# Odd attention: four weight groups in every second step in place of two in each

## The chip, the cores and the metric

The kernel runs on one NeuronCore of one Trainium2 chip. The metric is device time in microseconds (us) of one execution, the median over several runs of the same program. Everything is fp32 outside; inside, the big products are made from pairs of fp32r operands (a head and a tail), three matmuls each.

The engines are named as the profile names them: PE is TensorE's matmul, PEld its weight load, DVE is VectorE, ACT ScalarE, POOL GpSimd, SP the queue that loads the weights from memory.

## The reference, cut to what matters

A two-layer trunk on one sequence of 512 tokens, 1024 features. Layer 0 ("even") mixes with gated DeltaNet and differential attention, layer 1 ("odd") with 16-head attention, and each has a gated MLP behind it. The change touches the odd layer's attention only:

```
h = rmsnorm(x, odd_norm_mix)
cq, ck, cv = split_cols(h @ odd_w_qkv, (1024, 1024, 1024))      # 16 heads of 64
# chunks of 64 tokens; each attends to its own chunk and the 8 before it: here all that came earlier
s = einsum("bqhd,bkhd->bhqk", q_c, k_b) * 64**-0.5 + bias
p = softmax(where(valid, s, -inf))
o = einsum("bhqk,bkhd->bqhd", p, v_b)
x = x + o_c @ odd_w_out
```

With 512 tokens the band of nine chunks reaches everything before, so the mask is block-causal. In blocks of 128 queries, block b (0 to 3) has (b + 1) * 128 keys.

## The kernel before

**Pairs and steps.** The 16 heads go as eight pairs (pair 0 to pair 7). `attention("odd", i, ...)` on each engine handles one pair: eight score tiles, item t = (head m = t % 2, query block b = t // 2), and four blocks of the product with the values. PE runs twelve steps, t = 0 to 11:

- t < 8: the scores s_t, two matmuls (L846, L847) with 128, 256, 384 or 512 columns, into bank R0 for even t and R1 for odd t. DVE reads them, adds the bias and takes the maximum (L1655); ACT takes the exponential (L1183); DVE multiplies by the reciprocal sum, which gives the tile `pn` (L1684, L1689).
- t = 1: `vt`, four transposes of the value tile `vf` (L853) into bank R2. ACT copies them to `av` (L1187).
- t >= 2: `t{z}` with z = t - 2, that is z // 2 + 1 transposes of `pn` (L863), into bank R2 as well. ACT copies each to `pT` (in the trace `pT` or `qr`, L1195). Bank R2 has one user at a time: the transposes of z wait for ACT's copy of z - 1.
- even t >= 4: the values' product of block (t - 4) // 2 (L874) into bank R3.

In the text below tr_z stands for the transposes of item z.

**The fill.** While a pair's attention runs, PE also computes the next pair's projection q, k, v, as 24 *groups* of three matmuls with 512 columns (L619, L620, L621), one group for each of the eight slices of the 1024 inputs and each of three output tiles. They come from a generator, `features`; `run(fill, n)` takes the next n groups. Before the change each step t < 8 runs two groups and each step from 8 on one; what is left runs behind step 11. For pair 7 the fill is the output projection's first 21 groups (`out_terms`, tiles oh, ol). Inside a step the order is: scores, vt, fill, transposes, values' product. Each engine executes its own queue strictly in the order of the program, with semaphores between the engines.

**What the start of a pair waits for.** At steps 8 and 9 and behind step 9, ACT and DVE empty the next pair's projection: DVE writes `aq`, `ak`; ACT splits the next weights (`wh`, L373), DVE their tails (`wl`, L377); ACT writes `qs` and `kh` (L1087 to L1089), DVE `qs`'s tails, one for each head of the pair (L1384, x2, semaphore `q_tail`), POOL `kl` (L549, `k_tail`); and then DVE writes `vf` (L1413, semaphore `acc_free1`). The scores s_0 and s_1, which belong to different heads, each wait for their own head's tails, and vt waits for `vf`. Behind `vf` DVE writes the previous pair's `ol` and a weight tail, and only then reads s_0.

Of the kernel before, what the change touches and what calls it, by code (L numbers as in the profile page):

```python
# [157 lines left out]
def build(nc, T, out):  # L158

    ctx = ExitStack()  # L160
    with ctx:
# [5 lines left out]
        def sem(name):  # L167
            if name not in sems:
                sems[name] = ctx.enter_context(nc.semaphore(name))
            return sems[name]  # L170
# [170 lines left out]
        def read(eng, phase, job, i):  # L341

            b, n = BANK.use(phase, job, i)
            eng.wait_ge(sem(f"R{b}_read"), n + 1)
# [262 lines left out]
        def _(pe):  # L607
            def job(phase, name, i, first=True):
                b, n = BANK.use(phase, name, i)
                if not (isinstance(n, int) and n == 0):  # L610
                    pe.wait_ge(sem(f"R{b}_read"), n)
                return R[b]

            def done(ins, phase, name, i):
                b, _ = BANK.use(phase, name, i)
                ins.then_inc(sem(f"R{b}_full"), 1)
# [33 lines left out]
            def run(gen, n=1000):  # L650
                for _ in range(n):
                    if next(gen, 0) == 0:
                        return

            def token_sums(r, c0, squares):

                for b in range(NB):
                    last = nc.tensor.matmul(r[:, c0 + b:c0 + b + 1], squares[:, b * P:(b + 1) * P], ones[:, 0:1],  # L658
                                            start=True, stop=True)
                return last  # L660
# [161 lines left out]
            def rope_products(i):  # L822
                for n, nm_ in enumerate(("rot_q", "rot_k")):
                    pe.wait_ge(sem("acc_free0"), 2 * i + (2 * UNIT["diff"] + n + 3))
                    r = job("diff", nm_, i)
                    done(nc.tensor.matmul(r[:, :], cblk(C_PERM), qr[n][:, :], start=True, stop=True),
                         "diff", nm_, i)

            def attention(ph, i, fill, more=True):

                diff = ph == "diff"
                items = [(m, b) for b in range(NB) for m in (0, 1)]
                o = None
                per = 4 if diff else 8
                for t in range(8 + 4):
                    if t < 8:
                        m, b = items[t]
                        r = job(ph, f"s{t}", i)
                        if b == 0:
                            n = i if diff else i + NH  # L840
                            if m == 0:
                                pe.wait_ge(sem("kl_zero"), 2 if diff else 4)
                            for name in ("q_tail", "k_copy", "k_tail"):
                                pe.wait_ge(sem(name), 2 * n + (m + 1))
                        w = slice(0, (b + 1) * P)
                        nc.tensor.matmul(r[:, w], qs[m][:, b * P:(b + 1) * P], kh[m][:, w], start=True, stop=False)  # L846
                        done(nc.tensor.matmul(r[:, w], qs[m][:, b * P:(b + 1) * P], kl[m][:, w], start=False,  # L847
                                              stop=True), ph, f"s{t}", i)
                    if t == 1:
                        pe.wait_ge(sem("acc_free1"), 2 * i + (2 * UNIT[ph] + 2))  # L850
                        r = job(ph, "vt", i)
                        for b in range(NB):
                            last = nc.tensor.transpose(r[:, b * P:(b + 1) * P], vf[:, b * P:(b + 1) * P], ident)  # L853
                        done(last, ph, "vt", i)
                    run(fill, 2 if t < 8 else 1)

                    z = (t - 3) // 2 if diff and (t - 3) % 2 == 0 else t - 2 if not diff else -1
                    if 0 <= z < per:
                        b = z if diff else items[z][1]
                        pe.wait_ge(sem("pn_" + ph), per * i + z + 1)  # L860
                        r = job(ph, f"t{z}", i)
                        for k in range(b + 1):
                            last = nc.tensor.transpose(r[:, k * P:(k + 1) * P], pn[z % 2][:, k * P:(k + 1) * P], ident)  # L863
                        done(last, ph, f"t{z}", i)

                    b = (t - 4) // 2 if t % 2 == 0 else -1
                    if 0 <= b < NB:
                        if o is None:
                            o = job(ph, "pv", i)
                        read(pe, ph, f"t{b if diff else 2 * b + 1}", i)  # L870
                        for k in range(b + 1):
                            for m in (0,) if diff else (0, 1):
                                rows_ = slice(0, P) if diff else half[m]
                                last = nc.tensor.matmul(o[rows_, b * P:(b + 1) * P], av[:, k, rows_],  # L874
                                                        pT[2 * m + b % 2][:, k * P:(k + 1) * P],
                                                        start=(k == 0), stop=(k == b))
                        if b == NB - 1:
                            done(last, ph, "pv", i)
                        else:
                            last.then_inc(sem("pv_" + ph), 1)  # L880
                    if t == 9 and diff and more:
                        rope_products(i)
                run(fill)
                if diff:
                    pe.wait_ge(sem("sqo_diff"), i + 1)
                    r = job(ph, "oc", i)
                    done(token_sums(r, 0, osd), ph, "oc", i)
                    pe.wait_ge(sem("do_diff"), i + 1)
                    r = job(ph, "ro", i)
                    done(nc.tensor.matmul(r[:, :], ones, osd[:, :], start=True, stop=True), ph, "ro", i)  # L890
# [71 lines left out]
            with pe.Fori(0, NH - 1) as i:  # L962
                attention("diff", i, attn_units(i + (UNIT["diff"] + 1)))

            def heads_wait(k):
                pe.wait_ge(sem("oc_tail" if k < NH else "o_tail"), k % NH + 1)

            attention("diff", NH - 1, out_terms(UNIT["out0"], (0, 1, 2, 4, 5, 6, 3), KD - 1, heads_wait), more=False)
            out_rest(UNIT["out0"], KD - 1, heads_wait)
            mlp_layer(0, 1)  # L970
# [6 lines left out]
            with pe.Fori(0, NPAIR - 1) as i:  # L977
                attention("odd", i, attn_units(i + (UNIT["odd"] + 1)))
# [857 lines left out]
```

## Time and profile before

| | us |
|---|---|
| median of 3 runs | 1458.46 (1452.70 to 1458.87) |
| the profiled execution, whole | 1460.56 |
| its span | 1458.9 |
| PE busy | 1391.2 (95%) |
| DVE busy | 843.6 (58%) |
| ACT busy | 619.7 (42%) |
| POOL busy | 181.2 (12%) |
| mean granted clock of PE | 0.964 |

The span is what the profiler saw between the first and the last instruction; the whole execution's time is 1.7 us longer. Odd attention, steps 0 to 11 of eight pairs, takes from 834 us to some 1038 us of the span, 25.6 us a pair. In the timeline an instruction's row gives its start, its duration, engine, line, operation, tiles and shapes; where its engine stood idle before it, the idle time and who ended it follow in brackets. Matmuls overlap in the pipe, so the distance between two starts is what one costs, not its duration.

### The profile page before, as it was taken

What the parts mean: (1) busy time and instruction counts of PE and PEld (TensorE: products, weight loads), DVE (VectorE), ACT (ScalarE), POOL (GpSimd) and SP (SyncE); (2) the same over time, 40 slices, a digit from 0 to 9 for tenths busy, and PEclk for the clock granted to TensorE, in tenths of its full rate; (3) what the DMA queues carried; (4) which work ended last, traced back from release to release, by engine and by line L of the source; (5) the groups of instructions that cost most, each with busy time, mean ns of one, the idle gap of its engine ahead of it and who ended that gap; (6) DMA issues with size and microseconds to landing.
All of it is one profiled execution on the core that took longest, in us unless ns stands there. A gap on an engine that the chain in (4) does not pass through costs nothing.

```text
span 1458.9 us, 19831 instructions
## 1 busy us (share of the span) xinstructions
PE 1391.2 (95%) x6775; PEld 1138.7 (78%) x6775; DVE 843.6 (58%) x1235; ACT 619.7 (42%) x865; POOL 181.2 (12%) x177
## 2 busy tenths in 40 slices
PE   5979999899989999999999999999999999999996
PEld 4769878677767888888888777777778888888874
DVE  5666675566655666435555556667556664355542
ACT  4333232355543444223334566666444442233342
POOL 1031033011222100000001312122220000000011
PEclk9979979899989999999999999999999999999998
DMA  6421011012323642333313422324223323334132
GB/s 190 147 58 30 20 39 30 15 44 58 115 58 102 171 131 73 107 108 92 110 54 90 129 71 82 89 70 112 76 58 98 103 72 107 109 87 114 55 90 58
DMA packets 218642, 124.80 MB, mean 86 GB/s; under 512 B 6048, under 2 KB 215435, under 8 KB 218341
## 3 DMA queue, kind: packets, MB, share of 16 engines
q1 hardware_dynamic: 213744, 112.54, 27.4%
q0 software_dynamic: 3664, 11.58, 2.8%
q8 instruction: 29, 0.48, 0.1%
q10 hardware_dynamic: 1188, 0.08, 0.1%
q14 instruction: 17, 0.13, 0.0%
HBM read 119.94 MB, written 9.48 MB: 89 GB/s over the span
## 4 chain that ended last, share of the span: by engine, by line
PE 86%; DVE 5%; ACT 5%; issue 3%; DMA 1%; POOL 0%; ACTq 0%; DVEq 0%; SPq 0%; POOLq 0%
PE acc L619 24%; PE acc L620 23%; PE acc L621 23%; PE R L720 4%; ACT wh L373 2%; PE R L874 2%; PE R L863 1%; PE R L846 1%; PE R L658 1%; PE R L847 1%; PE R L740 1%; DVE wl L377 1%; DVE cta L1362 1%; PE R L718 1%; DMA xin<-in_x 1%
## 5 line engine op out<-in xcount | busy, mean ns | idle before, releaser
L619 PE MATMUL acc<-mh,wh 128*128 128x512 f32 x1120 | 456.4, 408 | 9.5 <-DVE ml L1315 5.4
L621 PE MATMUL acc<-mh,wl 128*128 128x512 f32 x1120 | 442.0, 395 | 0.0
L620 PE MATMUL acc<-ml,wh 128*128 128x512 f32 x1120 | 441.4, 394 | 0.0
L377 DVE TENSOR_TENSOR wl<-raw,wh 128x2048 fp32r<-128x2048 f32 x116 | 251.8, 2171 | 135.8 <-ACT wh L373 135.7
L373 ACT ACTIVATE wh<-raw 128x2048 fp32r<-128x2048 f32 x116 | 210.1, 1811 | 145.7 <-PE acc L621 144.3
L619 PEld LDWEIGHTS acc<-mh,wh 128*128 128x128 f32 x1120 | 213.9, 191 | 56.0 <-issue 9.2
L621 PEld LDWEIGHTS acc<-mh,wl 128*128 128x128 f32 x1120 | 213.1, 190 | 46.2
L620 PEld LDWEIGHTS acc<-ml,wh 128*128 128x128 f32 x1120 | 214.0, 191 | 41.5 <-issue 2.6
L494 POOL TENSOR_TENSOR ssum<-ssum,sq 128x512 f32<-128x512 f32 x32 | 52.0, 1624 | 716.8 <-ACT sq L1007 716.1
L619 PE MATMUL acc<-ah,wh 128*128 128x512 f32 x352 | 137.7, 391 | 0.4 <-DVE wl L377 0.3
L621 PE MATMUL acc<-ah,wl 128*128 128x512 f32 x352 | 137.0, 389 | 0.0
L620 PE MATMUL acc<-al,wh 128*128 128x512 f32 x352 | 137.0, 389 | 0.0
L1757 DVE SCALAR_TENSOR_TENSOR cta<-cb,pv,cta 128x512 f32<-128x512 f32 x88 | 66.2, 752 | 74.1 <-ACT cta L1254 67.7
L1183 ACT ACTIVATE pr<-ns,nm 128x128 f32<-128x128 f32 (+3 forms) x96 | 53.9, 561 | 76.3 <-DVE nm L1655 53.3
L1254 ACT ACTIVATE cta<-cb,pv 128x512 f32<-128x512 f32 x44 | 35.9, 817 | 103.8 <-DVE cb L1750 103.6
L619 PEld LDWEIGHTS acc<-ah,wh 128*128 128x128 f32 x352 | 66.0, 188 | 16.5 <-issue 2.3
L621 PEld LDWEIGHTS acc<-ah,wl 128*128 128x128 f32 x352 | 66.1, 188 | 14.0
L620 PEld LDWEIGHTS acc<-al,wh 128*128 128x128 f32 x352 | 66.1, 188 | 13.2
L1777 DVE TENSOR_TENSOR x<-x,acc 128x512 f32 (+1 forms) x32 | 22.0, 688 | 72.6 <-PE acc L621 72.3
L1260 ACT ACTIVATE ah<-pd 128x512 f32 x44 | 27.8, 632 | 69.6 <-DVE pd L1766 69.6
L1655 DVE CUSTOM_DVE_ANT_0 ns<-R,gb 128x128 f32<-128x128 f32 (+3 forms) x64 | 30.7, 489 | 44.6 <-PE R L847 44.6
L619 PE MATMUL acc<-oh,wh 128*128 128x512 f32 x128 | 53.3, 416 | 3.0 <-DVE ol L1719 3.0
(285 smaller groups left out, 1780.5 us busy)
## 6 DMA issues: line engine op xcount, KB each, us to landing
raw<-in_ffn_w_in SPq DMA_DIRECT2D x88, 512.0 KB, 5.0
raw<-in_even_w_in SPq DMA_DIRECT2D x24, 512.0 KB, 5.2
raw<-in_ffn_w_out SPq DMA_DIRECT2D x32, 384.0 KB, 4.1
raw<-in_ffn_w_out SPq DMA_DIRECT2D x32, 320.0 KB, 3.6
raw<-in_odd_w_qkv SPq DMA_DIRECT2D x16, 512.0 KB, 4.5
rel_bias_extended<-rel_bias_rows POOLq DMA_DIRECT2D x16, 320.0 KB, 4.0
raw<-in_even_w_out SPq DMA_DIRECT2D x8, 512.0 KB, 4.6
raw<-in_odd_w_qkv SPq DMA_DIRECT2D x16, 256.0 KB, 3.1
```

The costliest lines, as they stand in the source:

```text
L373: nc.scalar.activation(wh[s][:, 0:n], raw[s][:, 0:n], ACT.Copy).then_inc(sem(f"w_head{s}"), 1)
L377: nc.vector.tensor_tensor(wl[s][:, 0:n], raw[s][:, 0:n], wh[s][:, 0:n].bitcast(F32), ALU.subtract).then_inc(sem(f"w_tail{s}"), 1)
L494: pool.tensor_tensor(ssum[:, :], ssum[:, :], sq[s][:, :], ALU.add).then_inc(sem("ssum"), 1)
L619: nc.tensor.matmul(o, ah_, bh_, start=first, stop=False)
L620: nc.tensor.matmul(o, ah_, bl_, start=False, stop=False)
L621: return nc.tensor.matmul(o, al_, bh_, start=False, stop=last)
L720: last = nc.tensor.matmul(r[:, t], lhs, triu if b is triu else b[:, t], start=True, stop=True)
L874: last = nc.tensor.matmul(o[rows_, b * P:(b + 1) * P], av[:, k, rows_], pT[2 * m + b % 2][:, k * P:(k + 1) * P], start=(k == 0), stop=(k = ...
L1183: A(pr[t % 2][:, 0:w], ns[t % 2][:, 0:w], ACT.Exp, bias=nm[:, t:t + 1], scale=-1.0, accum_out=rs[:, t:t + 1]).then_inc(sem("exp_" + ph), 1)
L1254: A(cta[s][:, :], cb[s][:, ALPHA - 2:ALPHA - 2 + S], ACT.Identity, bias=pv[:, bass.ds(j + (PV_CB + JF * layer), 1)], scale=pv[:, bass.ds(j ...
L1655: free(V.tensor_tensor_reduce(out=ns[t % 2][:, 0:w], in0=r[:, 0:w], in1=bias, scale=-1.0, scalar=3e38, op0=ALU.add, op1=ALU.min, accum_out ...
L1757: V.scalar_tensor_tensor(out=cta[s][:, :], in0=cb[s][:, o:o + S], scalar=pv[:, bass.ds(j + (w0 + JF * tap), 1)], in1=cta[s][:, :], op0=ALU ...
```

## The change

The number of groups that a step takes from the fill. Before: two in each of the steps 0 to 7, one from step 8 on. After: for differential attention (`diff`) the same; for odd attention none in steps 0, 2, 4, 6, four in steps 1, 3, 5, 7, and one from step 8 on. The sum over the first eight steps stays 16.

```
-                    run(fill, 2 if t < 8 else 1)
+                    run(fill, 2 if diff and t < 8 else 1 if t >= 8 else 4 * (t % 2))
```

Only PE's queue changes; those of DVE, ACT, POOL and SP are the same. The start of a pair on PE, before (here pair 7, whose fill reads oh and ol; the other pairs read the same with mh and ml), from s_0's second matmul to s_2's first, with the semaphores that each waits for:

```order
L847 MATMUL R<-kl,qs 128x128
L619 MATMUL acc<-oh,wh 128x512 [waits R3_read,acc_free0,w_tail0]
...
L621 MATMUL acc<-oh,wl 128x512
L846 MATMUL R<-kh,qs 128x128 [waits k_copy,k_tail,q_tail,R1_read]
L847 MATMUL R<-kl,qs 128x128
L853 MATMUL R<-cst,vf 128x128 [waits R2_read,acc_free1]
L853 MATMUL R<-cst,vf 128x128 x3
L619 MATMUL acc<-oh,wh 128x512 [waits R3_read]
...
L846 MATMUL R<-kh,qs 128x256 [waits R0_read]
```

and after:

```order
L847 MATMUL R<-kl,qs 128x128
L846 MATMUL R<-kh,qs 128x128 [waits k_copy,k_tail,q_tail,R1_read]
L847 MATMUL R<-kl,qs 128x128
L853 MATMUL R<-cst,vf 128x128 [waits R2_read,acc_free1]
L853 MATMUL R<-cst,vf 128x128 x3
L619 MATMUL acc<-oh,wh 128x512 [waits R3_read,acc_free0,w_tail0]
...
L846 MATMUL R<-kh,qs 128x256 [waits R0_read]
L847 MATMUL R<-kl,qs 128x256
L863 MATMUL R<-cst,pn 128x128 [waits R2_read,pn_odd]
```

The two groups between s_0 and s_1 have moved behind vt, and the two between s_2 and tr_0 behind s_3. The second place is steps 3 and 4 on PE, from tr_1 to s_5, before:

```order
L863 MATMUL R<-cst,pn 128x128 [waits R2_read,pn_odd]
L846 MATMUL R<-kh,qs 128x384 [waits R0_read]
L847 MATMUL R<-kl,qs 128x384
L619 MATMUL acc<-oh,wh 128x512
...
L621 MATMUL acc<-oh,wl 128x512
L863 MATMUL R<-cst,pn 128x128 [waits R2_read,pn_odd]
L863 MATMUL R<-cst,pn 128x128
L874 MATMUL R<-pT,av 64x128 [waits R2_read,R3_read]
L874 MATMUL R<-qr,av 64x128
L846 MATMUL R<-kh,qs 128x384 [waits R1_read]
```

and after:

```order
L863 MATMUL R<-cst,pn 128x128 [waits R2_read,pn_odd]
L846 MATMUL R<-kh,qs 128x384 [waits R0_read]
L847 MATMUL R<-kl,qs 128x384
L863 MATMUL R<-cst,pn 128x128 [waits R2_read,pn_odd]
L863 MATMUL R<-cst,pn 128x128
L874 MATMUL R<-pT,av 64x128 [waits R2_read,R3_read]
L874 MATMUL R<-qr,av 64x128
L846 MATMUL R<-kh,qs 128x384 [waits R1_read]
L847 MATMUL R<-kl,qs 128x384
L619 MATMUL acc<-oh,wh 128x512
```

Between tr_1 and tr_2, which use bank R2 one after the other, two groups stood before; now only s_4 does. Steps 5 and 6 (tr_3, s_6, tr_4) moved in the same way.

## Rows read from the trace of the kernel before

**Rows 1.** One pair by window: length, busy time of each engine, granted clock, DMA
```profile
860.40:886.00 25.60, 25.44 (x154) 20.14 (x153) 16.87 (x41) 17.07 (x35) 5.57 (x7) 1.00 0.29 81
```

**Rows 2.** PE's waits in the odd stage: total us, times, longest
```profile
PE R L874 <- ACT qr L1195: 1.1, 7, 0.2
PE R L846 <- DVE nm L1655: 0.7, 1, 0.7
```

**Rows 3.** Timeline of PE, pair 1: start, us, engine, line, operation
```profile
860.47 0.22 PE L846 MATMUL R<-kh,qs 128*128 128x128 f32 x1
...
860.64 0.44 PE L619 MATMUL acc<-mh,wh 128*128 128x512 f32 x1
...
862.26 0.62 PE L853 MATMUL R<-cst,vf 128*128 128x128 f32 x4
...
867.42 0.27 PE L863 MATMUL R<-cst,pn 128*128 128x128 f32 x1
...
867.88 0.39 PE L619 MATMUL acc<-mh,wh 128*128 128x512 f32 x1
...
870.40 0.39 PE L619 MATMUL acc<-mh,wh 128*128 128x512 f32 x1
...
871.78 0.38 PE L863 MATMUL R<-cst,pn 128*128 128x128 f32 x2
...
872.47 0.39 PE L619 MATMUL acc<-mh,wh 128*128 128x512 f32 x1
```

**Rows 4.** Timeline of DVE, start of pair 1
```profile
857.73 3.36 DVE L1384 TENSOR_TENSOR qs<-aq,qs 64x512 fp32r<-64x512 f32 x2
861.13 0.69 DVE L1413 TENSOR_TENSOR vf<-acc,rstd 128x512 f32<-128x512 f32 x1
```

**Rows 5.** Timeline of ACT, pair 1
```profile
864.58 0.58 ACT L1187 ACTIVATE av<-R 128x512 f32<-128x512 f32 x1
...
867.72 0.28 ACT L1195 ACTIVATE qr<-R 128x128 f32<-128x128 f32 x1 [0.24 <-PE R L863]
...
872.20 0.39 ACT L1195 ACTIVATE qr<-R 128x256 f32<-128x256 f32 x1
...
879.08 1.91 ACT L373 ACTIVATE wh<-raw 128x2048 fp32r<-128x2048 f32 x1
880.88 0.59 ACT L1195 ACTIVATE qr<-R 128x512 f32<-128x512 f32 x1
```

**Rows 6.** Timeline of PE's weight loads: s_0 of pair 0, last values' product of pair 1
```profile
834.08 0.19 PEld L846 LDWEIGHTS R<-kh,qs 128*128 128x128 f32 x1 [1.08 <-DVE qs L1384]
...
881.52 0.13 PEld L874 LDWEIGHTS R<-pT,av 128*64 128x64 f32 x1 [0.59 <-ACT qr L1195]
```

**Rows 7.** Timeline of PE, start of pair 0
```profile
834.08 0.33 PE L846 MATMUL R<-kh,qs 128*128 128x128 f32 x1 [0.65 <-DVE qs L1384]
...
834.36 0.44 PE L619 MATMUL acc<-mh,wh 128*128 128x512 f32 x1
...
835.80 0.31 PE L846 MATMUL R<-kh,qs 128*128 128x128 f32 x1
...
836.58 0.66 PE L853 MATMUL R<-cst,vf 128*128 128x128 f32 x4 [0.36 <-DVE vf L1413]
```

**Rows 8.** Timeline of DVE, start of pair 0
```profile
835.76 0.69 DVE L1413 TENSOR_TENSOR vf<-acc,rstd 128x512 f32<-128x512 f32 x1
```

**Rows 9.** Timeline of ACT and of PE, step 2 of pair 7
```profile
1019.36 0.58 ACT L1187 ACTIVATE av<-R 128x512 f32<-128x512 f32 x1
...
1020.32 0.27 PE L863 MATMUL R<-cst,pn 128*128 128x128 f32 x1
```

**Rows 10.** Timeline of PE, between two heads of differential attention
```profile
319.28 1.12 PE L890 MATMUL R<-osd,cst 128*128 128x512 f32 x2 [1.37 <-DVE osd L1710]
```

**Rows 11.** Windows behind that pause, and at pair 0's start; columns as in Rows 1
```profile
321.00:327.00 6.00, 5.78 (x22) 4.63 (x23) 3.61 (x8) 4.44 (x7) 1.54 (x1) 0.72 0.46 114
834.00:838.00 4.00, 3.56 (x18) 2.83 (x19) 3.94 (x8) 2.06 (x3) 1.18 (x1) 1.00 0.94 255
```

## The prediction

> **What bounds the kernel now.** I read the windows first. In one pair of the odd attention PE is busy for 25.44 of 25.60 us at a granted clock of 1.00, the upper of its two levels, 2.4 GHz; DVE is busy for 16.87 us and ACT for 17.07 [rows 1]. The list of waits says the same from the other side: in the whole stage PE waits 0.16 us seven times for ACT ahead of the last values' product and once 0.7 us for DVE [rows 2]; beside these stand only the waits at pair 0's start [rows 7]. So PE sets the end here. It has no slack, and nothing behind the stage gives back what it loses: each us in which PE stands still is a us of the total. On the other hand there is next to nothing left for a rearrangement of PE's queue to win by taking waits away: 1.1 + 0.7 us and pair 0's 0.65 and 0.36 [rows 2, 7].
>
> Then I read the timelines of PE, DVE and ACT side by side, for what each step of PE needs from the others and how long before it is there. The change keeps all matmuls and takes away the cover between steps in four places of a pair. Those are the terms.
>
> **Price of a group.** From the first fill matmul of step 5 to tr_3 lie two groups: 870.40 to 871.78, 1.38 us [rows 3]. The number of groups is unchanged, so their work cancels in the sum; what counts is what stood still meanwhile.
>
> **Term 1: start of pairs 1 to 6.** DVE's queue is the late one. It splits the two heads' query tails until 857.73 + 3.36 = 861.09 and then writes vf from 861.13 to 861.82 [rows 4]. PE is at s_0 at 860.47 [rows 3]. Before, two groups lay between s_0 and s_1, and vt came at 862.26, when vf was done: no wait. After the change s_1 follows s_0 at once, needs the second head's tail and starts at about 861.15; vt behind it needs vf. What passes between vf's end and vt I take from pair 0, where vt did wait: vf ends at 835.76 + 0.69 = 836.45, vt starts at 836.58, 0.13 us [rows 7, 8]. So vt starts at 861.95. That is 0.31 earlier than the 862.26 of before, but two groups, which used to be done by then, are still to be done: 1.38 - 0.31 = 1.07 us a pair, 6.4 us for six pairs. Before, PE hid DVE's lateness behind weights; now it stands idle some 0.45 us ahead of s_1 and as much ahead of vt.
>
> Does DVE's chain come earlier, once PE's order is changed? It hangs on the split of the next weights on ACT at 879.08, queued behind ACT's copy of tr_6 [rows 5], and from step 8 on PE's order is the same. So the chain keeps its distance to PE's later steps. I take the whole 1.07.
>
> **What comes behind vt.** ACT copies vt to av until 864.58 + 0.58 = 865.16 [rows 5], behind the first two exponentials, and tr_0 waits for that copy, since both use bank R2. This copy does not move (it hangs on DVE's reading of s_0, which comes behind vf in DVE's queue). After the change PE is at tr_0 at about 861.95 + 0.4 (vt) + 2.8 (four groups) + 0.25 (s_2) = 865.4. That is covered, by 0.2 us.
>
> **Term 2: pair 0.** Here PE waits already: s_0 at 834.08, s_1 at 835.80 for the tail that follows two groups, vt at 836.58 behind a wait for vf [rows 7]. All three times are DVE's and stay; the two groups that used the gap go behind vt. Cost: 1.38 us.
>
> **Term 3: pair 7.** DVE has another weight tail to write ahead of s_0, so av is copied only at 1019.36 + 0.58 = 1019.94 [rows 9]. Vt is 0.31 earlier as in term 1, PE would be at tr_0 at about 1019.1 and has to wait till 1019.99, against 1020.32 before [rows 9]. From there to tr_1 it has two groups more than before: 1.38 - 0.33 = 1.05, and with a weight load that isn't hidden behind the wait (term 4) 1.1 us. The old wait of 0.7 ahead of s_2 [rows 2] vanishes in this.
>
> **Term 4: bank R2 at steps 4 and 6.** In step 4 tr_2 now follows tr_1 with only s_4 between. ACT copies tr_1 from 867.72 to 868.00 [rows 5], 0.30 after tr_1's start at 867.42; PE has done s_4 by 867.88, where its fill starts in rows 3. From a copy's end to PE's going on it takes 0.05 us: 880.88 + 0.59 = 881.47 [rows 5], weight load at 881.52 [rows 6]. So tr_2 may start at 868.05, a wait of 0.17. To that comes the weight load, which then stands in the open: s_0 with a wait takes 834.36 - 834.08 = 0.28 us to the next matmul, without one 860.64 - 860.47 = 0.17 [rows 3, 7], so 0.11 more. Together 0.28 us. Step 6: tr_3 is two blocks, copied from 872.20 to 872.59 [rows 5]; PE would be on at 872.47 [rows 3]; 0.17 again, 0.28 with the load. In step 2 the partner of tr_0 is vt (above), in step 8 a group still lies between. So 2 x 0.28 x 8 pairs = 4.5 us. If PE's load were ready at once, 0.17 x 16 = 2.7; if ACT were late too, by as much as the 0.24 it idled there [rows 5], 8.3.
>
> On the weight load the Trainium skill says, in "TensorE: Matmul & The Clock Gate", section "Step-by-step: what each phase is for", that PE's queue pulls weight loads ahead of matmuls in flight. By that rule a load would be ready when the wait ends, and the sum would be some 2 us smaller. The trace disagrees for a matmul that waits: the load of s_0 starts at 834.08 with its matmul, after 1.08 us of idle time [rows 6]. I go by the trace.
>
> **Small gains.** The first fill matmul behind small ones lasts 0.44 against 0.39 us [rows 3]. Four such switches a pair go away: 0.05 x 4 x 8 = 1.6 us at most, and where the scores before have 384 columns the row shows none (867.88, 0.39). I take 0 and keep 1.6 for the range. The scores and transposes cost the same by themselves in any order, as far as rows tell. Two scores now reach DVE close together; their tiles `pn` are wanted four groups (2.8 us) later at the earliest, against DVE operations of 0.3 to 0.7 us, so I put no cost on it.
>
> **Sum.** 6.4 + 1.4 + 1.1 + 4.5 = 13.4 us. The profiled execution took 1460.56 us, 1.7 more than its span, and is 2.1 above the runs' median of 1458.46. Forecast: 1460.56 + 13.4 = 1474.0 for a profiled execution, and 1458.46 + 13.4 = 1471.9, so 1472 us for the median, 0.9% slower. Its own range: terms 1 to 3 are 8.9; with 2.7 for term 4 and the full gain 10.0, so 1468.5; with 8.3 for term 4 1475.7. To this comes the spread of the runs themselves, whose lowest is 5.8 below the median.
>
> **Rival 1: the clock falls.** The new idle time comes in pieces of half a us at each pair's start, and at pair 0 as 0.65, about 1.4 and about 0.5 us within 3.2 us. In differential attention PE idles for 1.37 us at 319.28 [rows 10], shortly before its next scores, and behind that the granted clock averages 0.72 over 6 us, with part of it at the lower level of 1.2 GHz: (1 - 0.72) x 6 = 1.7 us lost [rows 11]. Against it: with 0.65 and 0.36 us idle at pair 0's start the granted clock stayed 1.00 [rows 7, 11]. Once at every pair's start would be 8 x 1.7 = 13.6 more, 1485.5. At pair 0 alone, 1.7 more, I count it in with the forecast. The Trainium skill has this case in the same page, section "A second HAM failure mode: psum-queue depth-cycling": short idle times between groups of matmuls, if frequent, make the clock go back and forth. By that rule the time would be this rival's; rows 1 show a steady 1.00 with frequent but very short waits, which doesn't decide it.
>
> **Rival 2: no slower, because the chain behind vf moves forward.** PE's fill to group 16 is ready for ACT and DVE as before, but scores 1, 3, 5 and 7 come earlier relative to the fill, so DVE and ACT finish the normalisations earlier. If thereby ACT's split at 879.08 and with it q_tail and vf came at least 1.1 us earlier relative to the pair's end, terms 1 to 3 would mostly vanish (-8.9), and term 4 less the gain at the switches would be left: 4.5 - 1.6 = 2.9, so 1461, within 0.5%; with copies of tr_1 and tr_3 in time as well, 1457. It decides at ACT's copy of tr_6: only if that comes earlier. Against it: this copy waits for PE's transposes of step 8, and those stay where they were.
>
> **Chances.** Forecast 0.77, rival 1 0.12, rival 2 0.11. Range for 8 times in 10: 1463 to 1479 us; below lie rival 2 and lucky runs, above rival 1. Against 1458.46, 0.5% is 7.3 us, about what a measurement can tell from no change. Slower by over 0.5% (above 1465.8): most of the forecast's cases and rival 1, 0.86; within 0.5%: 0.11, rival 2 and an overestimated term 1; faster: 0.03.
>
> **What would show it.** In the profile after: (a) a new wait ahead of L853 for `vf`, and one ahead of L846 for `qs`'s tails (L1384), eight times each, 0.4 to 0.6 us each, 1.4 at pair 0; (b) waits of L863 for ACT's L1195, sixteen, near 0.2 us; (c) one pair takes 25.6 + 1.1 + 0.56 = 27.2 us by window; (d) the wait of L846 for DVE's `nm` gone, and one of L863 for ACT's `av` copy in pair 7; (e) granted clock still 1.00 in the stage, or rival 1. The prediction is wrong if a pair takes less than 26.3 us, if vt doesn't wait, or if the rest of the span, outside the stage, changes by more than 2 us.

## The result, and the profile after

| | before | after |
|---|---|---|
| median of 7 runs each | 1458.5 us (1446.3 to 1459.8) | 1468.6 us (1462.4 to 1474.2) |
| ratio | | 1.0087 (95%: 1.0054 to 1.0119) |
| profiled execution, whole / span | 1460.56 / 1458.9 | 1474.15 / 1471.7 |
| from pair 0's s_0 to the last values' product of pair 7 | 834.08 to 1037.00: 202.9 us | 834.19 to 1051.21: 217.0 us |

The change makes the kernel slower, by 10 us in the medians (0.7%), 12.7 by the ratio and 14.1 in the stage itself, the last row of the table. Executions of one program differ by 12 to 14 us, nearly as much as the change costs. So below the stage and the length of one pair tell the experiments apart, and the ratios stand beside them.

One pair by window, pair 1, and the first four us behind pair 0's vt (length; busy time of PE, PEld, DVE, ACT, POOL; granted clock, DMA share, GB/s):

```profile
863.91:891.01 27.10, 26.21 (x153) 20.18 (x152) 16.93 (x41) 16.70 (x35) 5.51 (x7) 1.00 0.28 76
836.67:840.67 4.00, 4.00 (x13) 3.26 (x14) 1.86 (x7) 1.36 (x5) 0.00 (x0) 0.58 0.62 171
```

A pair takes 27.10 us against 25.60 in [rows 1]; DVE and ACT have the same work. Behind pair 0's start the granted clock is 0.58. The waits in the odd stage after (us in total, times, longest), against [rows 2]:

```profile
PE R L846 <- DVE qs L1384: 4.3, 9, 1.2
PE R L853 <- DVE vf L1413: 2.8, 8, 0.4
PE R L863 <- ACT av L1187: 0.9, 1, 0.9
PE R L863 <- ACT qr L1195: 0.2, 1, 0.2
PEld R L863 <- ACT qr L1195: 7.7, 21, 0.4
```

Each vt and each s_1 waits now. The waits of tr_2 and tr_4 for bank R2 show in the weight loads' list (PEld), which had seven such entries before and has 21 now; on PE itself all but one are too short to be listed. Before:

```profile
PEld R L863 <- ACT qr L1195: 2.2, 7, 0.3
```

The start of pair 1 on PE and on DVE, against [rows 3, 4]:

```profile
863.91 0.22 PE L846 MATMUL R<-kh,qs 128*128 128x128 f32 x1
...
864.59 0.33 PE L846 MATMUL R<-kh,qs 128*128 128x128 f32 x1 [0.34 <-DVE qs L1384]
...
865.39 0.65 PE L853 MATMUL R<-cst,vf 128*128 128x128 f32 x4 [0.36 <-DVE vf L1413]
...
868.86 0.27 PE L863 MATMUL R<-cst,pn 128*128 128x128 f32 x1
```

```profile
861.17 3.36 DVE L1384 TENSOR_TENSOR qs<-aq,qs 64x512 fp32r<-64x512 f32 x2
864.56 0.69 DVE L1413 TENSOR_TENSOR vf<-acc,rstd 128x512 f32<-128x512 f32 x1
```

s_1 starts 0.06 us behind the second tail's end (861.17 + 3.36 = 864.53), vt 1.48 us behind s_0; tr_0 at 868.86 doesn't wait. Steps 3 and 4 of pair 0 on PE, and the weight load of tr_2:

```profile
844.81 0.27 PE L863 MATMUL R<-cst,pn 128*128 128x128 f32 x1
844.84 0.42 PE L846 MATMUL R<-kh,qs 128*128 128x384 f32 x1
845.10 0.34 PE L847 MATMUL R<-kl,qs 128*128 128x384 f32 x1
845.45 0.44 PE L863 MATMUL R<-cst,pn 128*128 128x128 f32 x2
```

```profile
845.45 0.20 PEld L863 LDWEIGHTS R<-cst,pn 128*128 128x128 f32 x2 [0.33 <-ACT qr L1195]
```

tr_2 comes 0.64 us behind tr_1; without a wait PE was on after 0.46 [rows 3], so 0.18 of waiting. The weight load comes no earlier than its matmul. The start of pair 0, with its pauses and what they bring, against [rows 7]:

```profile
834.19 0.33 PE L846 MATMUL R<-kh,qs 128*128 128x128 f32 x1 [0.66 <-DVE qs L1384]
...
835.87 0.33 PE L846 MATMUL R<-kh,qs 128*128 128x128 f32 x1 [1.24 <-DVE qs L1384]
...
836.67 0.65 PE L853 MATMUL R<-cst,vf 128*128 128x128 f32 x4 [0.36 <-DVE vf L1413]
837.07 0.57 PE L619 MATMUL acc<-mh,wh 128*128 128x512 f32 x1
...
838.29 0.63 PE L619 MATMUL acc<-mh,wh 128*128 128x512 f32 x1
839.57 0.63 PE L619 MATMUL acc<-mh,wh 128*128 128x512 f32 x1
840.80 0.39 PE L619 MATMUL acc<-mh,wh 128*128 128x512 f32 x1
```

Three groups behind vt take 1.22, 1.28 and 1.23 us in place of 0.69: the lower of the two clock levels, 1.2 GHz. The first of them costs some 0.1 more than 0.69 at the upper level too, as two groups in this place show before the change (1.47 us against 1.38):

```profile
837.00 0.48 PE L619 MATMUL acc<-mh,wh 128*128 128x512 f32 x1
...
838.47 0.28 PE L846 MATMUL R<-kh,qs 128*128 128x256 f32 x1
```

So the clock loses 3.73 - 3 x 0.69 - 0.1 = 1.6 us; by the granted clock of the window above it is (1 - 0.58) x 4 = 1.7.

### The profile page after: what moved, and what is told of

It reads as the page before. It is cut to its first block, busy times and chain, and to the rows that moved or that the text cites. A ratio compares the mean times of both kernels' runs of the same rounds, so it can differ in the third digit from the quotient of the medians.

```text
span 1471.7 us, 19831 instructions
## 1 busy us (share of the span) xinstructions
PE 1398.3 (95%) x6775; PEld 1140.2 (77%) x6775; DVE 844.1 (57%) x1235; ACT 616.8 (42%) x865; POOL 180.5 (12%) x177
## 4 chain that ended last, share of the span: by engine, by line
PE 83%; DVE 7%; ACT 5%; issue 4%; DMA 1%; DVEq 0%; POOL 0%; ACTq 0%; SPq 0%; POOLq 0%
PE acc L619 23%; PE acc L620 23%; PE acc L621 23%; PE R L720 4%; ACT wh L373 2%; PE R L863 2%; DVE qs L1384 2%; PE R L874 1%; PE R L846 1%; PE R L658 1%; PE R L740 1%; DVE wl L377 1%; PE R L847 1%; DVE cta L1362 1%; PE R L718 1%
```

## The experiments

Each is run beside the kernel before on the same chip; the chip is not the same for all of them, so a median is compared with its own ratio and not with another experiment's median. "Pair" is the distance from one pair's s_0 to the next in pairs 1 to 6, "stage" the distance in the table above: 25.61 and 202.9 us before, 27.10 and 217.0 after.

### Start kept

```
-  run(fill, ... else 4 * (t % 2))
+  run(fill, ... else (2, 2, 0, 4, 0, 4, 0, 4)[t])
```

> Odd attention takes 2, 2, 0, 4, 0, 4, 0, 4 groups in steps 0 to 7: the start of a pair as before, the rest bunched as in the change. Theory A (the start of a pair costs 8.9 us and a clock drop at pair 0 some 1.5, bank R2 at steps 4 and 6 costs 3.7): no wait ahead of s_1 and vt, sixteen waits of L863 for ACT of some 0.17 us stay, one pair takes 25.61 + 0.46 = 26.07 us, total +3.7 us over before. Rival B (bunching itself costs, the same at each of the four bunches of a pair): three quarters of the loss stay, +9 to +10 us, one pair 26.7.

Measured: pair 27.00, stage 215.7, ratio 1.0059 (1.0041 to 1.0076), median 1464.4 us. Both expectations missed. The waits ahead of s_1 and vt are gone as theory A says, and a new one has taken their place. PE in step 2 of pair 1, and ACT beside it:

```profile
854.82 0.28 PE L846 MATMUL R<-kh,qs 128*128 128x256 f32 x1
...
855.93 0.33 PE L863 MATMUL R<-cst,pn 128*128 128x128 f32 x1 [0.71 <-ACT av L1187]
```

```profile
855.30 0.57 ACT L1187 ACTIVATE av<-R 128x512 f32<-128x512 f32 x1
```

tr_0 wants bank R2 as soon as s_2 is done, and ACT's copy of vt ends at 855.87, since it stands behind two exponentials that wait for DVE. With the start kept and step 2 emptied, only two groups are left between vt and tr_0; the change has four there. The prediction had this margin at 0.2 us for the change; I had not carried it over to this pattern. It is a third place where a pair's cover is thin.

Pair 7 shows a second cost. Up to the last values' product it takes 3.4 us more than before (pairs 1 to 6 take 1.4 more), and two pauses close together stand in it, with the lower clock behind them:

```profile
1017.67 0.39 PE L846 MATMUL R<-kh,qs 128*128 128x256 f32 x1 [0.68 <-DVE nm L1655]
...
1019.15 0.45 PE L863 MATMUL R<-cst,pn 128*128 128x128 f32 x1 [0.98 <-ACT av L1187]
```

```profile
1019.00:1023.00 4.00, 3.85 (x12) 3.22 (x13) 1.22 (x6) 1.49 (x6) 0.00 (x0) 0.57 0.87 235
```

By the granted clock of 0.57 that is (1 - 0.57) x 4 = 1.7 of the 3.4 us.

### Start only

```
+  run(fill, ... else (0, 4, 2, 2, 2, 2, 2, 2)[t])
```

> Odd attention takes 0, 4, 2, 2, 2, 2, 2, 2 groups: only the start of a pair is changed. Theory A: the waits ahead of s_1 and vt stay (vt 1.48 us behind s_0), those of tr_2 and tr_4 for bank R2 vanish, one pair 25.61 + 1.07 = 26.7 us, total +9 to +10.5 us over before, with the clock lower behind pair 0's start as with the change. Rival B: a quarter of the loss, +3 us, one pair 26.0.

Measured: pair 26.70 in the mean (26.73 and 26.67 in turn), stage 212.4, ratio 1.0048 (1.0031 to 1.0064), median 1465.2 us. The pair and the stage (+9.5) are as theory A says, and rival B's 26.0 is out. The whole time is 7 us over before by the ratio, somewhat under the +9 expected. The waits are the change's first two:

```profile
PE R L846 <- DVE qs L1384: 4.2, 9, 1.2
PE R L853 <- DVE vf L1413: 2.8, 8, 0.4
```

Pair 0 takes 29.28 us, with a granted clock of 0.57 in the four us that begin 3 us behind s_0.

### Odd transposes in bank R1

```
-ODD_JOBS = [(f"s{j}", j % 2) for j in range(8)] + [("vt", 2)] + [(f"t{j}", 2) for j in range(8)] + [("pv", 3)]
+ODD_JOBS = [(n, 1) for n in ("s1", "s3", "t1", "s5", "t3", "s7", "t5", "t7")] + [(f"s{j}", 0) for j in (0, 2, 4, 6)] \
+    + [("vt", 2)] + [(f"t{j}", 2) for j in (0, 2, 4, 6)] + [("pv", 3)]
```

> The change, and the transposes of odd items (t1, t3, t5, t7) go to bank R1 in place of R2, so that tr_2 and tr_4 need not wait for ACT's copy of tr_1 and tr_3. Theory A: those sixteen waits vanish, one pair 27.10 - 0.46 = 26.64 us, total 3.7 us below the change, +9 over before. Rival B: nothing changes, one pair 27.1. Rival C (scores s_5 and s_7 now wait for ACT's copies in R1): as much comes back there, one pair 27.1 with waits of L846.

This edit stands on top of the change. Measured: pair 26.60, stage 212.6, ratio 1.0038 (1.0018 to 1.0059), median 1463.6 us. The pair is as theory A says; the whole time is 5.5 us over before by the ratio, where 9 were expected, and the stage 9.7. In its list of waits the 7.7 us of weight loads behind L1195 are gone and no wait of the scores for ACT has come (rival C is out). 27.10 - 26.60 = 0.50 us a pair are bank R2's. Not all of it is new with the change: the last experiment finds 0.09 of it in the kernel before as well, so 0.41 are left for the waits of tr_2 and tr_4.

### Pair 0 kept

```
+  first = isinstance(i, int) and i == 0      # attention("odd", 0, ...) taken out of PE's loop
+  run(fill, 2 if (diff or first) and t < 8 else 1 if t >= 8 else 4 * (t % 2))
```

> The change in pairs 1 to 7, pair 0 with two groups a step as before. Theory A: pair 0 (from its s_0 to pair 1's s_0) takes 26.4 us again in place of 29.7 and its granted clock stays 1.00: two groups in the gap (1.38), two waits for R2 (0.46) and the clock (1.5) come back, total 3.3 us below the change. If the lower clock behind pair 0's start were chance of that one execution and not due to the longer pause, only 1.8 us come back against a run of the change with a steady clock.

Measured: pair 0 takes 26.27 us (29.72 with the change), the others 27.10, stage 213.5, ratio 1.0061 (1.0043 to 1.0079), median 1467.6 us. 3.5 us come back. The four us that begin 3 us behind pair 0's s_0, here and with the start only:

```profile
834.85:838.85 4.00, 4.00 (x21) 3.33 (x20) 2.51 (x14) 2.28 (x9) 0.00 (x0) 1.00 0.49 141
```

```profile
836.33:840.33 4.00, 4.00 (x13) 3.17 (x12) 1.35 (x7) 1.36 (x5) 0.00 (x0) 0.57 0.56 157
```

The same stretch shows 0.57 to 0.58 in all three profiles where pair 0 starts with three pauses of 0.65 or 0.66, 1.24 and 0.36 us (the change, start only, odd transposes in R1) and 1.00 in all nine others. So the lower clock comes with the pauses, not by chance.

### Half a weight tail

```
-  yield units_split_dve(dve, 0, g + 1)
+  yield units_split_dve(dve, 0, g + 1, 2 * ONE if diff else ONE)
```

> The change, with the fp32r tails of one of the two weight tiles (the k tile) left out in DVE's split (L377) while odd attention runs, so that this step takes 1.2 in place of 2.3 us; the values of k are wrong for it. Theory A (the start of a pair hangs on DVE's chain wl, qs tails, vf): the chain comes 1.1 us earlier, the wait ahead of s_1 vanishes, vf is then held by the end of the fill instead and vt starts about 1.0 us behind s_0 in place of 1.48: one pair 27.10 - 0.5 = 26.6 us. Rival D (the wait is for the end of the fill and its evacuation, not for DVE's chain): vt stays at 1.48, one pair 27.1.

This edit too stands on top of the change. Measured: pair 26.80, vt 1.19 us behind s_0, stage 213.2, one execution of 1463.1 us. The end of pair 0 and the start of pair 1 on PE, and DVE beside it:

```profile
854.42 0.39 PE L621 MATMUL acc<-mh,wl 128*128 128x512 f32 x1
854.64 0.22 PE L846 MATMUL R<-kh,qs 128*128 128x128 f32 x1
...
854.82 0.27 PE L846 MATMUL R<-kh,qs 128*128 128x128 f32 x1
...
855.83 0.65 PE L853 MATMUL R<-cst,vf 128*128 128x128 f32 x4 [0.62 <-DVE vf L1413]
```

```profile
855.00 0.69 DVE L1413 TENSOR_TENSOR vf<-acc,rstd 128x512 f32<-128x512 f32 x1 [1.78 <-PE acc L621]
```

s_1 no longer waits, and vf is now held by the last group of the fill, as expected; from the start of that group's last matmul to vf's it takes 0.58 us and not the 0.4 or so behind my 1.0, so vt comes at 1.19. So rival D is out, but DVE's chain is only 0.3 of the 1.07 us (27.10 - 26.80). DVE stands idle for 1.78 us ahead of vf here, so an even earlier chain would not bring back the rest: vt needs what the fill has just finished, and only other work on PE can cover that.

### The mirror

```
+  run(fill, ... else (4, 0, 4, 0, 4, 0, 4, 0)[t])
```

> The mirror: 4, 0, 4, 0, 4, 0, 4, 0 groups in steps 0 to 7. Same bunches, but the four groups lie between s_0 and s_1. Theory A: no wait ahead of s_1 and vt, none at pair 0 but s_0's, clock 1.00 there; R2 waits only for tr_1 behind tr_0 (s_3 between, some 0.3 to 0.4 us), since the values' product lies between tr_2 and tr_3: one pair 26.0 us, the stage +2 to +3.5 us over before. Rival B (bunching itself costs): one pair 27.1, stage +14.

Measured: pair 27.23, stage 215.2, ratio 1.0100 (1.0048 to 1.0152), median 1468.0 us. The start of a pair has no wait and the clock stays at 1.00, as expected, and still the pair is as long as rival B says. But it isn't bunching as such. From step 7 on in pair 2, PE (tr_5 and tr_6) and ACT:

```profile
903.54 0.49 PE L863 MATMUL R<-cst,pn 128*128 128x128 f32 x3
...
905.89 0.66 PE L863 MATMUL R<-cst,pn 128*128 128x128 f32 x4 [1.17 <-ACT qr L1195]
```

```profile
904.65 0.72 ACT L1183 ACTIVATE pr<-ns,nm 128x512 f32<-128x512 f32 x1 [1.67 <-DVE nm L1655]
...
905.37 0.47 ACT L1195 ACTIVATE qr<-R 128x384 f32<-128x384 f32 x1
```

s_7 comes right ahead of tr_5 here, and in ACT's queue the exponential of s_7 stands ahead of the copy of tr_5. The copy waits for DVE's pass over s_7 and for the exponential, and tr_6 for the copy: 1.17 us. From tr_5 to tr_6 it takes 905.89 - 903.54 = 2.35 us, and before the change 1.07:

```profile
876.82 0.49 PE L863 MATMUL R<-cst,pn 128*128 128x128 f32 x3
...
877.89 0.65 PE L863 MATMUL R<-cst,pn 128*128 128x128 f32 x4
```

That is 1.28 of the pair's 1.62 us. Of the rest some 0.2 are the wait of tr_1 for tr_0's copy, which follows 0.64 us behind tr_0 here. I had looked for PE's neighbours in bank R2 and not for what stands ahead of the copy in ACT's queue.

### Late bunches

```
+  run(fill, ... else (2, 2, 2, 2, 0, 4, 0, 4)[t])
```

> 2, 2, 2, 2, 0, 4, 0, 4 groups: bunched only from step 4 on. Theory A, with what the experiment on the kept start taught (tr_0 had only two groups behind vt there and waited 0.93 us for the av copy): vt and tr_0 lie as before, no wait there; only the sixteen R2 waits stay: one pair 25.61 + 0.5 = 26.1 us, stage +4. Rival E (the 27.0 of the kept start came from bunching and not from tr_0's wait for av): one pair near 27.

Measured: pair 26.03, stage 206.5, ratio 1.0042 (1.0015 to 1.0070), median 1461.1 us. As theory A says; 0.43 us a pair, 0.21 a wait. Rival E is out: the kept start's length, 27.00 - 26.03 = 0.97 us a pair more than here, came with tr_0's wait for av. Pair 0 takes 0.4 us more than before and pair 7 0.6; the stage is 206.5 - 202.9 = 3.6 us longer.

### Late bunches, odd transposes in bank R1, and the banks alone

The pattern 2, 2, 2, 2, 0, 4, 0, 4 with the edit of the banks, run twice, and the kernel before with the edit of the banks alone.

> The same 2, 2, 2, 2, 0, 4, 0, 4, and the transposes of odd items in bank R1. Theory A: no new wait at all, so this shows what bunching by itself does: one pair 25.61 us, or down to 25.5 if the first group behind small matmuls costs 0.05 us at each switch (two switches fewer). Rival B: above 25.9. Against before: the same within 0.1%.

> The kernel before (two groups in each step), only with the transposes of odd items in bank R1. If the 0.12 us a pair by which the late bunches with banks beat the kernel before (25.49 against 25.61) come from bank R2 (tr_6 waits 0.05 us for tr_5's copy before), one pair takes 25.5 to 25.56 here too. If they come from the two switches between groups and small matmuls that the bunches save, one pair takes 25.56 to 25.61 and the late bunches keep at least half of their gain.

> The late bunches with banks once more (2, 2, 2, 2, 0, 4, 0, 4; odd transposes in R1), beside the run with banks alone: one pair 25.49 us, stage 1.0 us under before, ratio to before 0.9984 as the first time or nearer to 1; it is the candidate for a faster version, and by the stage's 1.0 us it should not be more than 0.1% faster.

Measured with late bunches: pair 25.49 and 25.50, stage 201.9 both times, ratio 0.9984 (0.9960 to 1.0009) and 0.9979 (0.9964 to 0.9994), medians 1453.7 and 1454.1 us. With the banks alone: pair 25.52, stage 202.1, ratio 0.9997 (0.9981 to 1.0012), median 1455.1 us. The first scores of pairs 1 and 2, with late bunches and with the banks alone (the edit of the banks moves all lines on by one, so that the first matmul of the scores is L847 here):

```profile
849.46 0.22 PE L847 MATMUL R<-kh,qs 128*128 128x128 f32 x1
874.97 0.22 PE L847 MATMUL R<-kh,qs 128*128 128x128 f32 x1
```

```profile
854.39 0.22 PE L847 MATMUL R<-kh,qs 128*128 128x128 f32 x1
879.91 0.22 PE L847 MATMUL R<-kh,qs 128*128 128x128 f32 x1
```

Of the 0.12 us a pair by which the first beats the kernel before, 0.09 are the banks' and 0.02 or 0.03 the bunches'. So bunching by itself costs nothing and gives next to nothing: rival B is out. The expectation of at most 0.1% was missed both times, by ratios of 0.16% and 0.21%. The stage shows only 1.0 us, 0.07%, and 0.8 of it are there with the banks alone, whose ratio shows 0.03%; where the rest of the two ratios comes from stays open, since the edits leave the program outside the stage as it is. A version that is faster than before by more than 0.1% isn't shown.

## Why the prediction was right

Forecast 1472 us, measured 1468.6; forecast 0.9% slower, measured 0.87% by the ratio and 0.7% by the medians. Term by term, from the stage of the profiled executions and the experiments:

| term | forecast | measured | from |
|---|---|---|---|
| 1: start of pairs 1 to 6 | 6.4 | 6.5 | start only: (26.70 - 25.61) x 6 |
| 2: pair 0, two groups | 1.4 | 1.3 | start only: 29.28 - 26.39, less the clock's 1.6 |
| 3: pair 7 | 1.1 | 1.2 | tr_1 comes 9.10 us behind s_0, 7.93 before |
| 4: bank R2, sixteen waits | 4.5 | 3.6 | stage with late bunches: 206.5 - 202.9; with the banks: (217.0 - 212.6) - (202.9 - 202.1) |
| clock behind pair 0's start | "counted in" as 1.7, not summed | 1.6 | nine matmuls at 1.2 GHz |
| sum | 13.4 | 14.1 | stage 217.0 - 202.9 |

The measured terms add to 14.2. In pair 7 steps 4 and 6 cost 0.30 and 0.37 us, more than elsewhere. ACT copies tr_1 there as soon as in the other pairs, but tr_2 follows 0.14 us behind the copy's end and not 0.05; why stays open.

The mechanism was the forecast one, with its waits where the prediction looked for them: 0.34 and 0.36 us ahead of s_1 and vt (forecast 0.4 to 0.6), 1.24 at pair 0 (forecast 1.4), one for av in pair 7. That the sum is so near is in part luck, as two errors in it, at term 4 and at the clock, go against each other.

**Term 1** held: vt 1.48 us behind s_0, as worked out from pair 0's row of before, and a cost of 1.09 us a pair for 1.07. Its reason was told too simply. The prediction put vt's lateness down to DVE's chain alone. Half a weight tail showed that with an earlier chain vt still comes at 1.19, held by the end of the fill itself.

**What comes behind vt**: the cover of 0.2 us for tr_0 held in the change; the kept start showed what happens when it doesn't, a pause of 0.71 us on PE and 0.97 us a pair.

**Term 4** was right in mechanism and 0.06 us a wait too large (0.28 forecast, 3.6 / 16 = 0.22 measured). The wait was 0.18, as forecast (0.17), and what is left for the weight load in the open is about 0.04 for a transpose, not the 0.11 read off a pair of score matmuls. In the row of tr_2's weight load above, load and matmul start together at 845.45: the load of this waiting matmul is not pulled past its wait. The rule of the Trainium skill on weight loads pulled ahead ("TensorE: Matmul & The Clock Gate", "Step-by-step: what each phase is for") would have given no cost; the measured one lies between the rule's and the prediction's.

**The small gains**, put at 0 with 1.6 as a bound, are next to nothing: two switches fewer a pair gave 0.02 or 0.03 us. The bound was read off durations of 0.44 and 0.39 us, which are not what a matmul costs.

**Rival 1** came true at one place, pair 0, for about the price given (1.6 for 1.7). At the other pairs pauses of 0.34 and 0.36 us left the clock at 1.00. The prediction said that it counts this in at pair 0, but its sum of 13.4 has no such term; it should have been one. It is hardly missed in the total because term 4 was forecast too large by 0.9 and the medians moved by less than the stage. That is luck.

**Rival 2** did not happen: DVE reaches vf 0.65 us behind s_0 (864.56 - 863.91), as before (861.13 - 860.47).

**The medians** moved by less than the stage (10.1 against 14.1), the means of the same executions by 12.9. The profiled execution came out at 1474.15 us for a forecast of 1474.0; as the stage had grown by 14.1 and not 13.4 and what follows it took 1.4 us less than before, this is chance too. The start of the stage lies between 823 and 834 us in the twelve profiles, although PE's program is the same up to there, with a mean granted clock between 0.95 and 0.97 ahead of it; that spread is left in every execution's time and so in the medians.

## What to carry to other kernels

Where one engine sets the end and fills its waits with independent work, count for each dependent pair of operations how much of that work lies between them; moving it in larger pieces leaves the sum unchanged and takes the cover from some pairs. For each pair ask what the producer's engine has queued ahead of the result, and whether both use one buffer in turn; two patterns here that I had expected to be cheap each opened such a wait elsewhere (tr_0 for av, tr_6 for a copy behind an exponential). Pauses of a us or so close together on TensorE can cost a second time, by the clock: 1.6 us at pair 0.

## What the runs showed of the hardware

- Three pauses of 0.66, 1.24 and 0.36 us within 3.1 us had PE at its lower clock level behind them, for three groups, in three of three profiles (granted clock 0.57 over four us), and so did two pauses of 0.68 and 0.98 us within 2.2 us in pair 7 of the kept start, in one profile (0.57). Pauses of 0.65 and 0.36 us with two groups between them did not, in six, nor did 1.22 and 0.36 us, in the one profile with half a weight tail, nor 0.39, 0.27 and 0.92 us spread over 5.6 us in pair 7 of the change. Which of their sizes and distances decides was not tried.
- Changing only which PSUM bank the odd transposes use took 0.09 us a pair off the kernel before, although its list of PE's waits shows no transpose; the wait is visible in the weight loads' list alone (2.2 us in seven entries before, none with the banks alone), and tr_6's transposes are done 0.09 us earlier.
